# SyncE's order in the second recurrence: solved block out and back, next pair's blocks out, off-diagonal copies, blocks in

## The chip, the cores and the metric

The kernel runs on one core of a Trainium2 chip. Its time is the device time of one execution in microseconds. It was run three times, and the median counts. The profile is of one further execution, with its own time.

## What is computed

Batch 1, 512 positions, width 2048, float32. A first block (a modulated norm, a projection, sparse attention on 8 heads, a gated linear recurrence on 8 heads, an output projection) is followed by two layers: one of stick-breaking attention and pooling, and one whose core is this recurrence over time, on 32 heads of 64 channels:

```python
def step(state, inp):
    r_t, w_t, k_t, v_t, kk_t, a_t = inp
    sa = jnp.einsum('bhvk,bhk->bhv', state, -kk_t)
    state = (state * w_t[:, :, None, :]
             + sa[..., None] * (kk_t * a_t)[:, :, None, :]
             + v_t[..., None] * k_t[:, :, None, :])
    return state, jnp.einsum('bhvk,bhk->bhv', state, r_t)
```

It is the second recurrence of the title. A projection and a layer norm follow it. All else is unchanged and only takes its time before and after.

## The kernel before

Most of the kernel is matrix products: weights come from DRAM into `RAW`, ScalarE (ACT) and VectorE (DVE) split them in a high and a low part, and TensorE (PE) multiplies three times (L321 to L323). The second recurrence stands near the end, between the last group of such products and the output projection.

**Chunks and pairs.** Two heads make a pair of 128 channels, so there are 16 pairs (`PAIRS`), and the 512 positions are 8 chunks of 64. Within a chunk the update by `kk` and `a` couples the positions by a triangular 64 by 64 system, one for each chunk and head, so 16 systems in a pair. Each is inverted in three steps. First its four diagonal blocks of 16 by 16 are solved, by GpSimd (POOL). Then TensorE joins blocks of 16 to blocks of 32 ("level 5", l = 0 in `pe_level_w` and `pe_level_y`) and blocks of 32 to 64 ("level 6", l = 1), which takes the blocks next to the diagonal, copied out of the system to `T_N5` and `T_N6`. After that come products (`pe_pq`, `pe_fg`, `pe_oa`, `pe_gg`) and eight hops of the state from chunk to chunk (`pe_hop`, `dve_hop`).

**The systems' way.** `pe_nt` makes the systems of pair q in PSUM, and `act_nt` (L2105) copies them to SBUF and counts `nt_sb`. POOL works on another layout, one system to a partition, so everything goes over DRAM, all of it by DMAs that SyncE (SP) issues:
- `sp_blocks_out` (L1824) waits for `nt_sb` and writes the systems to `blocks_scratch` (2 DMAs);
- `sp_blocks_in` (L1830) waits until these have landed and reads the diagonal blocks to `SOLVE_IN` (2 DMAs);
- `pool_solve` waits for the solved block of the pair before to be out (`y_out`), sets the start (L1870), waits for the blocks (`n_in`) and runs 15 steps of two operations (L1876, L1879), the last of which counts `solved`;
- `sp_solved_out` (L1845) waits for `solved` and writes the solved block to `solved_scratch` (2 DMAs);
- `sp_solved_back` (L1851) waits until these have landed and reads them to `YT` in the layout of the products (2 DMAs); DVE's transpose `dve_inverse` (L2232) reads it next;
- `sp_levels` (L1839) waits for `w` (the level products of the pair before) and copies the blocks off the diagonal from the systems to `T_N5` (4 DMAs) and `T_N6` (2 DMAs).

Scratch tensors and `SOLVE_IN` have two buffers each; POOL's own working tiles have one.

**The order.** The loop is written out for iterations t, and each engine has a list of its own in which a step belongs to pair t, t+1 and so on: `at(t + 3, f, 1)` calls f for pair t+3 if that is a pair and at least 1. An engine goes through its list in order, and a wait stops all that is behind it. PE's list (`wv_pe`) begins with level 5's product of pair t+1 (L1956), has `pe_nt` of pair t+3 a few steps on, and the second L1956 (level 6) behind it. SP's list (`wv_sp`) has five entries an iteration, with 14 DMAs. Pair 0 goes through the five steps ahead of the loop, and pair 1's blocks go out and in at t = -2, where no other entry applies. The inputs of later pairs are loaded by ACT in its own list (L1801, L1808). POOL has only `pool_solve`, pair after pair.

Of the kernel before, what the change touches and what calls it, by code (L numbers as in the profile page):

```python
# [108 lines left out]
def wait(eng, sem, value):  # L109

    if not isinstance(value, int) or value > 0:
        eng.wait_ge(sem, value)
# [7 lines left out]
def build(nc, xT, positions, cols_d, mats_d, causal_i_d, rows_d, band_d, wpool_d, lora_d, lora1_d, kw_d, ada_d, gate_d, w_d, out):  # L120
    ctx = ExitStack()
    with ctx:
# [16 lines left out]
        at = (nc.sbuf_base + 31) // 32 * 32  # L139
# [1562 lines left out]
        def ws(i, n=1):  # L1702

            buf, first = ((WS, 0) if i < 48 else (X, 48) if i < 64 else (RAW[0], 64) if i < 68 else (GATE[i - 68], i)
                          if i < 70 else (WK, 54))
            return buf[:, (i - first) * SEQ:(i - first + n) * SEQ]
# [103 lines left out]
        def by_row(a, r):  # L1810

            return a.rearrange("(z y) -> z y", y=8 * DIAG)[:, r * 4 * DIAG:r * 4 * DIAG + CH * CH].rearrange(
                "z (p i) -> p z i", i=CH)

        def by_block(a):

            return a.rearrange("(x y) -> x y", y=DIAG)[:, 0:BASE16 * CH].rearrange("x (j i) -> x j i", i=CH)[
                :, :, 0:BASE16]

        def sp_blocks_out(sp, q):  # L1820

            sp.wait_ge(wv("nt_sb"), q + 1)
            for r in range(2):
                sp.dma_start(by_row(n_d[q % 2], r), ws(N_OF(q))[rows(r)].rearrange("p (z i) -> p z i", i=CH)  # L1824
                             ).then_inc(wv("n_out"), 16)

        def sp_blocks_in(sp, q):
            sp.wait_ge(wv("n_out"), 32 * (q + 1))
            for g in range(2):
                sp.dma_start(SOLVE_IN[q % 2][rows(g)], by_block(n_d[q % 2])).then_inc(wv("n_in"), 16)  # L1830

        def sp_levels(sp, q):

            wait(sp, wv("w"), 2 * q)
            for l, w in ((5, 16), (6, 32)):
                for b in range(P // (2 * w)):
                    at, to = b * 2 * w, (b * 2 * w) % CH + w
                    view = lambda i: ws(i)[at:at + w, :].rearrange("p (z i) -> p z i", i=CH)[:, :, to:to + w]
                    sp.dma_start(view(T_N5 if l == 5 else T_N6), view(N_OF(q))  # L1839
                                 ).then_inc(wv("levels" if l == 5 else "levels6"), 16)  # L1840

        def sp_solved_out(sp, v):
            sp.wait_ge(wv("solved"), v + 1)
            for g in range(2):
                sp.dma_start(by_block(y_d[v % 2])[:, g:BASE16:2, :], SOLVED[rows(g)]).then_inc(wv("y_out"), 16)  # L1845

        def sp_solved_back(sp, v):
            sp.wait_ge(wv("y_out"), 32 * (v + 1))
            wait(sp, wv("pq"), 2 * (v - 1))
            for r in range(2):  # L1850
                sp.dma_start(YT(v)[rows(r)].rearrange("p (z i) -> p z i", i=CH), by_row(y_d[v % 2], r)  # L1851
                             ).then_inc(wv("y_in"), 16)

        def at(p, f, first=0):

            if first <= p < PAIRS:
                f(p)

        def wv_sp(sp, t):
            at(t + 3, lambda q: sp_blocks_out(sp, q), 1)  # L1860
            at(t + 2, lambda q: sp_solved_out(sp, q), 1)
            at(t + 3, lambda q: sp_blocks_in(sp, q), 1)
            at(t + 2, lambda q: sp_solved_back(sp, q), 1)
            at(t + 2, lambda q: sp_levels(sp, q), 1)

        def pool_solve(pool, v):

# [476 lines left out]
        def _(sp):  # L2344
# [81 lines left out]
            for t in range(-2, PAIRS):  # L2426
                wv_sp(sp, t)
# [748 lines left out]
```

## Time and profile before

| | us |
|---|---|
| median of three runs | 3448.85 |
| lowest and highest | 3445.24, 3454.91 |
| profiled execution, its time | 3452.13 |
| profiled execution, its span | 3450.4 |
| TensorE busy | 3308.2 |
| POOL busy | 423.9 |

The span is from the first to the last instruction in the profile. Busy is the time in which an engine works on an instruction; waits and the issuing of DMAs are not in it. In the profile "SPq" is SyncE issuing, "ACTq" ScalarE issuing.

### The profile page before, as it was taken

To read this page: it belongs to the slowest core of one execution; us is meant where nothing else is said; L and a number is where in the kernel's file an instruction comes from. 1 tells how busy PE (TensorE), PEld (TensorE's weight loads), DVE (VectorE), ACT (ScalarE), POOL (GpSimd) and SP (SyncE) were. 2 spreads that over 40 slices of the span, in tenths; PEclk is the share of its full clock that TensorE was granted. 3 is DMA by queue.
4 is the path that set the end of the run, shared out by engine and by line. 5 is a ranking of instruction groups with operands and counts; after the bars stand their busy time and mean duration, and the time that the engine had idled before them with its cause. 6 is when DMAs were issued, how large, how long until landed. Compare 5 with 4: busy or idle time off the path is not lost.

```text
span 3450.4 us, 51304 instructions
## 1 busy us (share of the span) xinstructions
PE 3308.2 (96%) x20966; PEld 2682.0 (78%) x20966; DVE 1844.9 (53%) x2416; ACT 1356.9 (39%) x1587; POOL 423.9 (12%) x804
## 2 busy tenths in 40 slices
PE   6999999999999999999999999999999997889897
PEld 1678888888887888888888867888888886777785
DVE  7666666666667233444423456242456435667545
ACT  2343544443444133444422236242445533444323
POOL 0001223132221000000000000000010113434000
PEclk9999999999999999999999999999999998999898
DMA  9422232233322432222222314444464555554321
GB/s 387 164 79 93 88 106 94 88 114 105 109 100 89 165 134 86 85 81 86 80 88 104 123 55 159 146 138 140 161 233 161 213 176 142 124 135 105 134 98 73
DMA packets 200156, 435.18 MB, mean 126 GB/s; under 512 B 114608, under 2 KB 118064, under 8 KB 166192
## 3 DMA queue, kind: packets, MB, share of 16 engines
q1 hardware_dynamic: 153536, 311.00, 26.6%
q0 software_dynamic: 21872, 77.67, 6.6%
q10 hardware_dynamic: 24576, 44.05, 4.0%
q8 instruction: 127, 2.08, 0.2%
q14 instruction: 45, 0.37, 0.0%
HBM read 370.80 MB, written 60.29 MB: 125 GB/s over the span
## 4 chain that ended last, share of the span: by engine, by line
PE 88%; DVE 5%; ACT 2%; issue 1%; DMA 1%; SPq 1%; ACTq 1%; POOLq 1%; DVEq 0%; POOL 0%
PE PJ L321 18%; PE PJ L323 18%; PE PJ L322 18%; PE AB L321 6%; PE AB L323 6%; PE AB L322 6%; PE AB L1956 1%; PE AB L1965 1%; PE PJ L1977 1%; PE AB L2027 1%; DMA WK<-ada 1%; PE PJ L1892 1%; PE AB L256 1%; PE AB L495 1%; PE AB L547 1%
## 5 line engine op out<-in xcount | busy, mean ns | idle before, releaser
L321 PE MATMUL PJ<-XH,WH 128*128 128x512 f32 x2816 | 1112.2, 395 | 15.0 <-DVE XL L469 7.6
L323 PE MATMUL PJ<-XH,WL 128*128 128x512 f32 x2816 | 1098.9, 390 | 0.0
L322 PE MATMUL PJ<-XL,WH 128*128 128x512 f32 x2816 | 1098.7, 390 | 0.0
L354 DVE TENSOR_TENSOR WL<-RAW,WH 128x2048 fp32r<-128x2048 f32 (+1 forms) x234 | 539.2, 2304 | 639.4 <-ACT WH L350 635.4
L350 ACT ACTIVATE WH<-RAW 128x2048 fp32r<-128x2048 f32 (+1 forms) x236 | 449.4, 1904 | 783.7 <-PE PJ L323 547.6
L321 PEld LDWEIGHTS PJ<-XH,WH 128*128 128x128 f32 x2816 | 530.1, 188 | 125.5 <-issue 17.5
L323 PEld LDWEIGHTS PJ<-XH,WL 128*128 128x128 f32 x2816 | 529.8, 188 | 111.8
L322 PEld LDWEIGHTS PJ<-XL,WH 128*128 128x128 f32 x2816 | 530.3, 188 | 108.7 <-issue 2.2
L321 PE MATMUL AB<-XH,WH 128*128 128x512 f32 (+1 forms) x960 | 380.0, 396 | 11.6 <-DVE XL L469 7.6
L323 PE MATMUL AB<-XH,WL 128*128 128x512 f32 (+1 forms) x960 | 375.3, 391 | 0.0
L322 PE MATMUL AB<-XL,WH 128*128 128x512 f32 (+1 forms) x960 | 375.2, 391 | 0.0
L321 PEld LDWEIGHTS AB<-XH,WH 128*128 128x128 f32 (+1 forms) x960 | 179.2, 187 | 55.2 <-issue 11.5
L322 PEld LDWEIGHTS AB<-XL,WH 128*128 128x128 f32 (+1 forms) x960 | 179.3, 187 | 41.9 <-issue 2.4
L323 PEld LDWEIGHTS AB<-XH,WL 128*128 128x128 f32 (+1 forms) x960 | 179.2, 187 | 40.1 <-issue 0.8
L659 POOL TENSOR_TENSOR TBL<-GATE,SMALL 128x512 f32<-128x512 f32 x16 | 30.3, 1892 | 485.5 <-PE AB L674 242.8
L663 POOL TENSOR_TENSOR TBL<-TBL,GATE 128x512 f32<-128x512 f32 x48 | 79.6, 1659 | 77.6 <-issue 76.2
L487 DVE COPY WK<-PJ 128x1024 f32<-128x1024 f32 x30 | 36.7, 1224 | 90.9 <-PE PJ L323 90.9
L256 PE MATMUL AB<-WK,SMALL 128*1 128x512 f32 x128 | 63.4, 635 | 21.9 <-DMA WK<-ada 21.8
L2481 POOL DMA_DIRECT2D TBL<-wpool x4 | 2.2, 546 | 593.0 <-DVE X L1376 444.4
L1876 POOL TENSOR_TENSOR X<-X 128x30 f32<-128x30 f32 (+10 forms) x240 | 66.9, 279 | 60.8 <-DMA X<-blocks_scratch 27.7
L1879 POOL TENSOR_TENSOR X<-X 128x30 f32<-128x30 f32 (+10 forms) x240 | 69.9, 291 | 35.2 <-issue 1.9
L1956 PE MATMUL AB<-WS 64*64 64x64 f32 x1024 | 39.7, 232 | 26.1 <-DVE WS L2242 10.9
(537 smaller groups left out, 3932.7 us busy)
## 6 DMA issues: line engine op xcount, KB each, us to landing
RAW<-w SPq DMA_DIRECT2D x232, 1024.0 KB, 4.8
WK<-ada SPq DMA_DIRECT2D x32, 1024.0 KB, 6.7
GATE<-gate POOLq DMA_DIRECT2D x64, 256.0 KB, 2.9
rkvg_scratch<-WK POOLq DMA_DIRECT2D x16, 1024.0 KB, 5.0
factors_scratch<-WK POOLq DMA_DIRECT2D x48, 256.0 KB, 2.9
X<-factors_scratch ACTq DMA_DIRECT2D x35, 256.0 KB, 4.0
x_scratch<-X POOLq DMA_DIRECT2D x8, 1024.0 KB, 5.7
rates_scratch<-WK POOLq DMA_DIRECT2D x16, 512.0 KB, 4.6
```

The lines of the kernel that those rows point to most:

```text
L256: m = nc.tensor.matmul(AB[0:1, 2 + b, :], SILU[:, SKT * k + j:SKT * k + j + 1], WK[:, at:at + SEQ], start=k == 0 and j == 0, stop=False)
L321: nc.tensor.matmul(bank[0:width, n, :], hi, xh, start=first, stop=False)
L322: nc.tensor.matmul(bank[0:width, n, :], hi, xl, start=False, stop=False)
L323: m = nc.tensor.matmul(bank[0:width, n, :], lo, xh, start=False, stop=last)
L350: nc.scalar.activation(WH[k % 2][:, :, 0:w], narrow(RAW[k % 2], w), ACT.Copy).then_inc(wh_ready, 1)
L354: nc.vector.tensor_tensor(WL[k % 2][:, :, 0:w], narrow(RAW[k % 2], w), WH[k % 2][:, :, 0:w].bitcast(F32), ALU.subtract).then_inc(wl_ready, 1)
L487: nc.vector.tensor_copy(WK[:, n0 * SEQ:n1 * SEQ].rearrange("p (b n) -> p b n", n=SEQ), PJ[:, n0:n1, :]).then_inc(evac_d, 1)
L495: m = nc.tensor.transpose(dst[:, t * P:(t + 1) * P], src[:, t * P:(t + 1) * P], mat("ident"))
L663: m = nc.gpsimd.tensor_tensor(GATE_ACC, GATE_ACC, GATE[k % 2][:, :], ALU.add)
L1876: P_TT(SCRATCH[:, 0:c, 0:w], n[:, j:j + 1, j + 1:].to_broadcast([P, c, w]), SOLVED[:, 0:c, j:j + 1].to_broadcast([P, c, w]), ALU.mult)
L1879: m = P_TT(SOLVED[:, 0:c, j + 1:], SOLVED[:, 0:c, j + 1:], SCRATCH[:, 0:c, 0:w], ALU.subtract)
L1956: i = nc.tensor.matmul(tok(bank(4), r, m, h), tok(ws(T_N6 if l else T_N5), r, m, h), tok(ws(T_X), r, m, h), start=True, stop=True)
```

## The change

SP's five entries of an iteration come in another order. What each does, waits for and counts is as before, and so are the steps ahead of the loop and all other engines' lists.

```diff
         def wv_sp(sp, t):
+            at(t + 2, lambda q: sp_solved_out(sp, q), 1)
+            at(t + 2, lambda q: sp_solved_back(sp, q), 1)
             at(t + 3, lambda q: sp_blocks_out(sp, q), 1)
-            at(t + 2, lambda q: sp_solved_out(sp, q), 1)
+            at(t + 2, lambda q: sp_levels(sp, q), 1)
             at(t + 3, lambda q: sp_blocks_in(sp, q), 1)
-            at(t + 2, lambda q: sp_solved_back(sp, q), 1)
-            at(t + 2, lambda q: sp_levels(sp, q), 1)
```

## Rows read from the trace of the kernel before

**Rows 1.** The page: the chain that ended last, by engine.

```profile
PE 88%; DVE 5%; ACT 2%; issue 1%; DMA 1%; SPq 1%; ACTq 1%; POOLq 1%; DVEq 0%; POOL 0%
```

**Rows 2.** A window: length, busy PE, PEld, DVE, ACT, POOL, clock, DMA, GB/s.

```profile
2820.00:3223.00 403.00, 347.70 (x7578) 298.27 (x7580) 252.14 (x429) 160.05 (x284) 144.97 (x500) 0.94 0.49 122
```

**Rows 3.** The chain of waits: start, length, piece, in us.

```profile
3011.21 0.93 PE AB L1956 x32
...
3053.70 2.09 issue
...
3206.78 1.07 PE AB L1956 x32
```

**Rows 4.** POOL in order of time: operations that begin or end a solve.

```profile
2869.71 0.21 POOL L1876 TENSOR_TENSOR X<-X 128x15 f32<-128x15 f32 x1 [11.01 <-DMA X<-blocks_scratch]
...
2882.92 0.22 POOL L1879 TENSOR_TENSOR X<-X 128x8 f32<-128x8 f32 x1
...
2890.10 0.21 POOL L1876 TENSOR_TENSOR X<-X 128x15 f32<-128x15 f32 x1 [0.39 <-DMA X<-blocks_scratch]
...
2901.34 0.22 POOL L1879 TENSOR_TENSOR X<-X 128x8 f32<-128x8 f32 x1
...
3191.59 0.22 POOL L1879 TENSOR_TENSOR X<-X 128x8 f32<-128x8 f32 x1
```

**Rows 5.** Waits in the loop (in total, times, longest); last L2232's own (in total, times).

```profile
SPq L1824 <- ACT WS L2105: 113.2, 14, 10.4
...
POOL X L1870 <- DMA solved_scratch<-X: 100.9, 13, 11.6
...
POOL X L1876 <- DMA X<-blocks_scratch: 16.3, 13, 2.8
...
PE AB L1956 <- issue: 7.7, 4, 2.2
...
  DMA WS<-solved_scratch: 6.8, 1
```

**Rows 6.** SP's issues in order of time: start, length, line, DMA, count.

```profile
2852.62 1.30 SPq L1845 DMA_DIRECT2D solved_scratch<-X  x2
2858.37 1.29 SPq L1851 DMA_DIRECT2D WS<-solved_scratch  x2
2859.70 1.31 SPq L1824 DMA_DIRECT2D blocks_scratch<-WS  x2
2865.39 1.31 SPq L1830 DMA_DIRECT2D X<-blocks_scratch  x2
...
2890.67 3.90 SPq L1839 DMA_DIRECT2D WS<-WS  x6
...
3016.41 1.30 SPq L1824 DMA_DIRECT2D blocks_scratch<-WS  x2
...
3025.98 4.51 SPq L1839 DMA_DIRECT2D WS<-WS  x6
...
3191.84 1.30 SPq L1845 DMA_DIRECT2D solved_scratch<-X  x2
3196.23 1.28 SPq L1851 DMA_DIRECT2D WS<-solved_scratch  x2
```

**Rows 7.** Landing of one DMA, of L1845 (solved out), then L1830 (blocks in).

```profile
DMA to landing us min/median/max: 2.1/3.9/6.6
...
DMA to landing us min/median/max: 2.5/3.5/5.1
```

**Rows 8.** Windows of three iterations, and of one iteration's first 2 us.

```profile
3033.45:3055.79 22.34, 19.12 (x480) 16.40 (x475) 16.97 (x30) 10.05 (x19) 9.56 (x32) 0.98 0.58 145
3055.79:3080.71 24.92, 21.87 (x478) 18.96 (x479) 16.26 (x28) 9.85 (x18) 8.73 (x30) 0.88 0.51 120
3146.47:3166.72 20.25, 19.11 (x484) 16.50 (x482) 16.31 (x30) 9.85 (x19) 9.54 (x32) 1.00 0.43 96
...
3055.00:3057.00 2.00, 1.21 (x23) 1.25 (x25) 0.00 (x0) 0.00 (x0) 1.14 (x5) 0.50 0.06 14
```

## The prediction, made before the changed kernel ran

> **What bounds the kernel now.** I read the page first, then the stretch of the second recurrence by windows, POOL's and SyncE's (SP's) instructions in order of time, the waits, and last the chain of waits. The chain that ended last lies 88% on TensorE [rows 1]. That average says little of the edited loop. The second recurrence runs from 2820 to 3223 us, 403 of 3450 us, with TensorE busy 347.7 us, POOL 145.0 us, and the DMA engines at half their share [rows 2]. The edit touches nothing outside it.
>
> Inside it the reader is to see two circles. The first is the compute circle, from one first L1956 (level 5's product) to the next, through PE, DVE and ACT: 22.34 us in a middle iteration (3033.45 to 3055.79), 20.25 us in a late one (3146.47 to 3166.72) where the loads of later pairs have ended [rows 8]. The second is the solve circle: SP carries a pair's blocks to DRAM and back, POOL solves them, SP carries the solved block out and back. POOL's solve takes 13.4 us for pair 1 (2869.71 to 2883.14) and 11.5 for pair 2 (2890.10 to 2901.56) [rows 4]. Its mean comes from the waits: between the ends of solve 2 and of solve 15 (3191.81) POOL idles 100.9 us until a solved block is out and 16.3 until blocks are in, 13 times each [rows 4, 5]; (290.25 - 117.2) / 13, less a copy of 0.3 us, is 13.0 us. So POOL is idle 40% of this stretch. The fourteen solves after solve 1 end on average 22.05 us apart, (3191.81 - 2883.14) / 14 [rows 4]: they keep the compute circle's pace and have slack. SP has slack too: in 14 waits it stands 113.2 us for ACT's copy of the systems, `nt_sb` [rows 5], which in the order of before is ahead of everything, the solved block included. But that block's return is not late: DVE's L2232, its first reader, waits for it once, 6.8 us [rows 5]. What is nearly late is the off-diagonal copies, SP's last step. PE stops 7.7 us in four places before L1956 with no releaser in the trace [rows 5], 2.09 us of them at 3053.70 [rows 3], and I count these as waits for those copies, the only input of L1956 that a DMA brings in itself.
>
> **The change, part by part.** No instruction is added or taken away: SP issues the same 14 DMAs an iteration, each now behind others.
>
> *Solved out and back come ahead of the wait for `nt_sb`.* They can leave when POOL ends. Nothing waits for them today, so this is worth 0.
>
> *Blocks out goes behind the wait for the solved block to land, and blocks in goes last.* This is what counts. In the order of before the next pair's blocks are already on their way while the solved block is, and blocks in is issued ahead of the wait for that landing. In the new order all that lies between two solves stands in one line. From the end of one solve to the end of the next:
> 1. Solved out issued and landed: 5.4 us. Rows: 5.75 (2852.62 to 2858.37), and 4.4 with no loads about (3191.84 to 3196.23) [rows 6]; the second DMA leaves 0.65 after the first and lands 2.1 / 3.9 / 6.6 us later [rows 7], so at most 7.3. I stay near the first row, because most iterations have loads beside them.
> 2. Solved back, two issues: 1.3 us [rows 6]. SP doesn't wait for its landing.
> 3. Blocks out, two issues: 1.3 us [rows 6]. `nt_sb` is there: it comes 5.2 us after L1956 begins (3011.21 to 3016.41) [rows 3, 6], and that L1956 begins some 12 us after the solve before.
> 4. Off-diagonal copies, six issues: 4.5 us (3.9 at 2890.67) [rows 6]. Their wait for `w`, on an L1956 a few us after the iteration's first, is also long past. They cover the landing of blocks out: that took 5.7 us from issue to blocks in (2859.70 to 2865.39) [rows 6], against 1.3 + 4.5 = 5.8 here.
> 5. Blocks in, until POOL's first operation: 4.4 us. Rows: 4.3 (2865.39 to 2869.71) [rows 4, 6]; 0.65 and a landing of 2.5 / 3.5 / 5.1 [rows 7] make 3.2 / 4.2 / 5.8.
> 6. The solve: 13.0 us; 11.5 to 13.4 [rows 4].
>
> The sum is 29.9 us. With the low end of each it is 4.4 + 1.3 + 1.3 + 3.9 + 4.2 + 11.5 = 26.6, with the high end 7.3 + 1.3 + 1.3 + 4.5 + 5.8 + 13.4 = 33.6. The trace of before holds one such circle, at the loop's start, where nothing overlaps yet: solved out 2852.62, solved back 2858.37, blocks out 2859.70, blocks in 2865.39, the solve until 2883.14 [rows 4, 6]. That is 30.5 us, without step 4 but with a full landing of 5.7 us in place of steps 3 and 4. It is the row nearest to my sum.
>
> This circle sets the pace then: 29.9 against 22.05 us. It begins after solve 1, since pair 1's blocks go out and in as before. Fourteen circles: 14 x 7.85 = 109.9 us.
>
> *The end.* From the last solve (3191.81) to the last first-L1956 (3206.78) it takes 15.0 us today, because compute is late there [rows 3, 4]. Then SP will be: 4.4 + 1.3, four of the six copies issued in 2.6, and a landing of 2 to 4 us [rows 6, 7], 11 in all: a gain of 4.0.
>
> *What the new idle time costs.* TensorE ends an iteration's work and stands some 5 us before each first L1956. Its granted clock is 0.50 (1.2 GHz) at 3055 to 3057, behind the stop of 2.09 us, and 0.88 in the mean over that iteration, so it came back to 2.4 GHz within it [rows 3, 8]. The iteration took 24.92 against 22.34 us before it, so 2.6 us [rows 8]. Beside a circle of 29.9 that is hidden; it would count if the circle were under 25. In the last iteration nothing hides it: + 2.4.
>
> Sum: 109.9 - 4.0 + 2.4 = 108.3 us; the profiled execution's 3452.1 + 108.3 = 3560.4. The median of the runs shown is 3.3 us below that execution, so I say **3557**.
>
> The rows above show no pair of solved-out DMAs that landed in under 4.4 us from the first issue. The Trainium skill ("DMA: Bandwidth & Descriptors", Anatomy of one DMA) gives a DMA a fixed cost of about 2 us, mostly the receipt of its last write. By that, steps 1 and 5 would take 2.65 us each, the circle would be 25.4, and the whole some 3496. No run here shows that for such short runs of data; a result near it falls below the range.
>
> **The rivals.**
> - *A short circle.* DMAs that today share the queues land alone. For it: the 4.4 us of the last solved out, the 11.5 of solve 2. Against: the loads of later pairs are still there in most iterations, and the circle at the start took 30.5. With every low end: 14 x (26.6 - 22.05) - 2 = + 62, so 3511.
> - *Compute on the slow clock throughout.* If the clock never came back, TensorE, busy 19.1 of the 20.25 us [rows 8], would need twice as long. With three quarters of the circle on it, that makes 35 us an iteration, 14 x 13 = + 182, so 3631. Against: the clock came back within one iteration after the stop [rows 8]. The Trainium skill ("TensorE: Matmul & The Clock Gate", Part 1) calls the throttled state the default, lifted by activity; if a busy share of 19 us in 30 didn't lift it, this is the case that follows.
> - *Faster: the copies come in time.* They leave right behind blocks out instead of 9.6 us after it (3016.41 to 3025.98) [rows 6]. If POOL's side keeps pace, the four stops before L1956 go, 7.7 us [rows 5], and with each 2.6 us of slow clock [rows 8]: - 18, so 3431. It decides at a circle of 22.05 us. Even the low ends miss it by 4.5; the solve would have to take 5 us instead of 13.
> - *No change.* The circle comes to about 22.5 us and its loss equals that gain. The same speaks against it.
>
> **How the numbers follow.** Forecast (a circle of 28 to 33 us) 0.83; short circle 0.07; slow clock 0.05; faster 0.03; no change 0.02. The last two bounds are at 0.3% (10 us), which is about what a measurement of this kernel tells from no change: slower 0.95, same 0.02, faster 0.03. The range: a circle of 27.3 us gives 3519 by the same sum, one of 32.3 gives 3589. I take 3514 to 3590, which leaves most of both outer rivals out.
>
> **What would show it.** In the profile after, solves end 28 to 33 us apart. POOL idles some 17 us between two solves, 5 before L1870 and 11 to 12 before L1876, for blocks coming in. SP's wait at L1824 for `nt_sb` is gone, and it waits for POOL at L1845 some 16 us each time. L1956 waits for the copies in every iteration, and the mean granted clock of the stretch falls under 0.94. Outside it nothing moves by over 2 us. The prediction is wrong if POOL starts solves less than 14 us after the last ended, or if iterations stay near 22 us.

## The result

The changed kernel took 3548.32 us (median of four runs, 3546.14 to 3550.76), the one before 3451.88 us on the same chip (the three runs above and a fourth): a ratio of 1.0276, with a 95% interval of 1.0248 to 1.0305. It is slower by some 96 us; 3557 was forecast, in 3514 to 3590. The profiled execution has a span of 3545.8 us, 95.4 more than before.

The page of the changed kernel, the chain that ended last, by engine, answers to [rows 1]:

```profile
PE 79%; DMA 5%; POOLq 4%; DVE 3%; SPq 3%; issue 3%; ACT 1%; DVEq 0%; ACTq 0%; POOL 0%
```

The chain has left TensorE for 9% of the span. Where it went is seen in the same view, of one circle between two solves' ends:

```profile
by line: POOLq L1878 18.6%; POOLq L1875 16.8%; issue 15.0%; SPq L1839 12.8%; DMA solved_scratch<-X 12.1%; DMA X<-blocks_scratch 10.8%; SPq L1824 4.4%; SPq L1851 4.2%; SPq L1845 4.2%; SPq L1830 2.1%; POOL X L1879 1.6%
```

Not one piece of it is TensorE's. The chain is POOL's solve, then each of SP's steps and two transfers. SP's issues in order of time, of that circle, answer to [rows 6]:

```profile
3032.47 1.29 SPq L1845 DMA_DIRECT2D solved_scratch<-X  x2
3036.64 1.27 SPq L1851 DMA_DIRECT2D WS<-solved_scratch  x2
3037.95 1.31 SPq L1824 DMA_DIRECT2D blocks_scratch<-WS  x2
3039.30 3.90 SPq L1839 DMA_DIRECT2D WS<-WS  x6
3043.25 1.34 SPq L1830 DMA_DIRECT2D X<-blocks_scratch  x2
3061.27 1.29 SPq L1845 DMA_DIRECT2D solved_scratch<-X  x2
```

POOL beside it, and the last operations of solve 1 and of solve 15, answer to [rows 4]:

```profile
2888.25 0.22 POOL L1879 TENSOR_TENSOR X<-X 128x8 f32<-128x8 f32 x1
...
3036.67 0.29 POOL L1870 COPY X<-MAT 128x128 f32<-128x128 f32 x1 [4.23 <-DMA solved_scratch<-X]
3047.19 0.21 POOL L1876 TENSOR_TENSOR X<-X 128x15 f32<-128x15 f32 x1 [10.23 <-DMA X<-blocks_scratch]
3061.03 0.22 POOL L1879 TENSOR_TENSOR X<-X 128x8 f32<-128x8 f32 x1
...
3289.59 0.22 POOL L1879 TENSOR_TENSOR X<-X 128x8 f32<-128x8 f32 x1
```

From solve 1 (2888.47) to solve 15 (3289.81) it is 28.67 us a circle, against 22.05. The waits answer to [rows 5], the first four of POOL and PE from 2900 to 3295, SP's and DVE's of the whole loop:

```profile
POOL X L1876 <- DMA X<-blocks_scratch: 149.8, 14, 11.8
...
PE AB L1956 <- issue: 56.8, 10, 8.4
...
POOL X L1870 <- DMA solved_scratch<-X: 51.4, 13, 5.9
...
PE AB L1956 <- DVE WS L2232: 14.2, 3, 5.2
...
SPq L1845 <- POOL X L1879: 243.1, 15, 17.0
SPq L1851 <- DMA solved_scratch<-X: 41.8, 16, 4.4
...
SPq L1824 <- ACT X L2105: 6.3, 1, 6.3
SPq L1830 <- DMA blocks_scratch<-WS: 6.3, 3, 4.7
...
  DMA WS<-solved_scratch: 60.7, 15
```

SP's 113 us of waiting for `nt_sb` are gone (the one left is ahead of the loop). It waits for POOL in their place, 16.2 us each time. POOL waits for its blocks, 10.7 us each time. TensorE stops ahead of the first L1956 in all fifteen iterations. The view puts three of the thirteen stops shown down to DVE's L2232, which reads the solved block, but L2232 had ended 0.7 to 0.9 us earlier there. The last of level 5's four copies lands 0.09 us ahead of L1956 in fourteen iterations and 0.14 us in the first: in the circle above it is issued at 3041.31 and lands 1.8 us later, and L1956 starts at 3043.21. So all these stops are waits for the copies. The windows answer to [rows 2, 8]:

```profile
2820.00:3320.00 500.00, 385.62 (x7719) 333.45 (x7721) 258.79 (x435) 164.11 (x292) 155.78 (x500) 0.84 0.40 99
...
3044.00:3046.00 2.00, 2.00 (x29) 1.76 (x25) 0.16 (x1) 0.60 (x1) 0.00 (x0) 0.50 0.49 53
3046.00:3048.00 2.00, 2.00 (x20) 1.76 (x20) 1.07 (x3) 0.60 (x1) 0.53 (x3) 0.50 0.30 28
...
3050.00:3052.00 2.00, 1.47 (x52) 1.23 (x44) 1.83 (x4) 0.84 (x2) 1.23 (x5) 1.00 0.00 0
```

The granted clock of the stretch fell from 0.94 to 0.84, because each iteration begins behind a stop of TensorE: L1956 starts at 3043.21 at 1.2 GHz and the clock is 2.4 GHz again from 3050.

### The profile page after: what moved, and what is told of

It is laid out like the page before. It is cut to its first block, busy times and chain, and to the rows that moved or that the text cites. A ratio compares the mean times of both kernels' runs of the same rounds, so it can differ in the third digit from the quotient of the medians.

```text
span 3545.8 us, 51304 instructions
## 1 busy us (share of the span) xinstructions
PE 3343.5 (94%) x20966; PEld 2713.4 (77%) x20966; DVE 1846.7 (52%) x2416; ACT 1356.4 (38%) x1587; POOL 434.0 (12%) x804
## 4 chain that ended last, share of the span: by engine, by line
PE 79%; DMA 5%; POOLq 4%; DVE 3%; SPq 3%; issue 3%; ACT 1%; DVEq 0%; ACTq 0%; POOL 0%
PE PJ L321 17%; PE PJ L323 17%; PE PJ L322 17%; PE AB L321 6%; PE AB L322 6%; PE AB L323 6%; POOLq L1878 2%; POOLq L1875 2%; DMA solved_scratch<-X 2%; DMA X<-blocks_scratch 1%; SPq L1839 1%; DMA WK<-ada 1%; SPq L1851 1%; SPq L1824 1%; PE AB L495 1%
## 5 line engine op out<-in xcount | busy, mean ns | idle before, releaser
L1956 PE MATMUL AB<-WS 64*64 64x64 f32 x1024 | 51.8, 274 | 87.7 <-issue 59.2
L1956 PEld LDWEIGHTS AB<-WS 64*64 64x64 f32 x1024 | 47.2, 184 | 92.8 <-issue 66.6
L1876 POOL TENSOR_TENSOR X<-X 128x30 f32<-128x30 f32 (+10 forms) x240 | 74.9, 312 | 194.3 <-DMA X<-blocks_scratch 161.1
L1879 POOL TENSOR_TENSOR X<-X 128x30 f32<-128x30 f32 (+10 forms) x240 | 72.4, 301 | 35.3 <-issue 1.9
```

Of the source, the lines that this page charges most:

```text
L1876: P_TT(SCRATCH[:, 0:c, 0:w], n[:, j:j + 1, j + 1:].to_broadcast([P, c, w]), SOLVED[:, 0:c, j:j + 1].to_broadcast([P, c, w]), ALU.mult)
L1879: m = P_TT(SOLVED[:, 0:c, j + 1:], SOLVED[:, 0:c, j + 1:], SCRATCH[:, 0:c, 0:w], ALU.subtract)
L1956: i = nc.tensor.matmul(tok(bank(4), r, m, h), tok(ws(T_N6 if l else T_N5), r, m, h), tok(ws(T_X), r, m, h), start=True, stop=True)
```

## The experiments

Each experiment but e4 and e5 moves entries of SP's list, and each ratio is to the kernel before on the same chip. "Circle" is the mean over the fourteen solves after solve 1, from end to end; "solve" is the mean of POOL's own part. Both are read from the profiled execution, the time from all runs.

| run | order after the exchange | us | ratio (95%) | circle | solve |
|---|---|---|---|---|---|
| before | blocks out, solved out, blocks in, back, copies | 3448.9 to 3458.5 | 1 | 22.05 | 12.9 |
| changed | solved out, back, blocks out, copies, blocks in | 3548.3 | 1.0276 (1.0248 to 1.0305) | 28.67 | 13.7 |
| e1 | solved out, back, blocks out, blocks in, copies | 3530.0 | 1.0231 (1.0214 to 1.0249) | 28.04 | 12.6 |
| e2 | blocks out, solved out, back, copies, blocks in | 3521.0 | 1.0197 (1.0180 to 1.0214) | 27.22 | 13.8 |
| e3 | solved out, blocks out, blocks in, back, copies | 3476.1 | 1.0070 (1.0053 to 1.0087) | 23.94 | 12.8 |
| e4 | as changed, 5 of 15 solve steps | 3441.2 | 0.9951 (0.9937 to 0.9965) | 20.92 | 4.2 |
| e5 | as before, 5 of 15 solve steps | 3457.4 | 1.0005 (0.9991 to 1.0019) | 21.93 | 4.0 |
| e6 | blocks out, solved out, blocks in, 4 copies, back, 2 copies | 3485.2 | 1.0086 (1.0057 to 1.0114) | 24.79 | 12.5 |
| e7 | blocks out, solved out, 4 copies, blocks in, back, 2 copies | 3463.5 | 1.0025 (1.0008 to 1.0043) | 23.12 | 13.5 |
| e8 | blocks out, 4 copies, solved out, blocks in, back, 2 copies | 3440.0 | 0.9951 (0.9932 to 0.9970) | 21.26 | 13.7 |
| e9 | blocks out, 6 copies, solved out, blocks in, back | 3453.6 | 1.0000 (0.9981 to 1.0020) | 21.87 | 13.7 |

**e1: do the copies cost, or only cover?** Against the changed kernel:

```diff
-            at(t + 2, lambda q: sp_levels(sp, q), 1)
             at(t + 3, lambda q: sp_blocks_in(sp, q), 1)
+            at(t + 2, lambda q: sp_levels(sp, q), 1)
```

> The changed order with its last two entries exchanged: blocks in ahead of the off-diagonal copies. My theory: the copies stand in the circle but cover the landing of blocks out (some 5.5 us from issue), so that blocks in can't leave sooner: solves 28.2 to 29.3 us apart (28.7 changed), time 3540 to 3560. Rival, that the six copies' issues (4.1 us) are themselves what blocks in waits for: solves 24.6 us apart, time near 3491.

The circle is just under the range and the time 10 us under it, far from the rival's 24.6 and 3491. Blocks in leaves on average 4.8 us after blocks out, where it left after 5.8 with the copies between: they cover most of the landing, but are not free by 1.0 us. What is gained there, blocks in loses on its way (4.7 us to POOL's first operation in place of 3.9, with the copies issued right behind it), and solved out lands 0.5 us later. The solve is 1.1 us shorter, for which the last section has the likely cause. Fourteen circles shorter by 0.63 us make 9 us. The two profiled executions are 18.9 us apart; another 7.0 of these lie ahead of the end of solve 1, which the exchanged entries don't touch, and 3.2 behind solve 15.

**e2: only blocks in last.** Against the changed kernel:

```diff
+            at(t + 3, lambda q: sp_blocks_out(sp, q), 1)
             at(t + 2, lambda q: sp_solved_out(sp, q), 1)
             at(t + 2, lambda q: sp_solved_back(sp, q), 1)
-            at(t + 3, lambda q: sp_blocks_out(sp, q), 1)
             at(t + 2, lambda q: sp_levels(sp, q), 1)
             at(t + 3, lambda q: sp_blocks_in(sp, q), 1)
```

> Order: blocks out, solved out, solved back, copies, blocks in. Blocks out leaves early as before; only blocks in stays behind the solved block's way and the copies. Theory (a serial circle): only the two issues of blocks out leave it, 28.7 - 1.35 = 27.3 us, time near 3529 (3515 to 3540). Rival, that what costs is blocks out standing behind the wait for the solved block to land: then the loss goes with it, 22 to 23 us, 3450 to 3465.

27.22 us against 27.3 forecast: from solved back to blocks in it takes 5.8 us in place of 7.2, and nothing else moves by over 0.3 us. SP's issues in one circle of it, in order of time:

```profile
3026.56 1.25 SPq L1845 DMA_DIRECT2D solved_scratch<-X  x2
3030.35 1.27 SPq L1851 DMA_DIRECT2D WS<-solved_scratch  x2
3031.66 3.90 SPq L1839 DMA_DIRECT2D WS<-WS  x6
3035.61 1.33 SPq L1830 DMA_DIRECT2D X<-blocks_scratch  x2
3043.23 1.29 SPq L1824 DMA_DIRECT2D blocks_scratch<-WS  x2
3053.87 1.25 SPq L1845 DMA_DIRECT2D solved_scratch<-X  x2
```

Blocks out waits beside the solve here and costs nothing; what stands between solved out and blocks in does. The rival's 22 to 23 us are far off.

**e3: the landing not waited for.** Against the kernel before:

```diff
+            at(t + 2, lambda q: sp_solved_out(sp, q), 1)
             at(t + 3, lambda q: sp_blocks_out(sp, q), 1)
-            at(t + 2, lambda q: sp_solved_out(sp, q), 1)
             at(t + 3, lambda q: sp_blocks_in(sp, q), 1)
```

> Order: solved out, blocks out, blocks in, solved back, copies. Solved out is first as in the change, but its landing isn't waited for ahead of blocks in. Theory: the circle is 1.3 (solved out) + 5.2 (blocks out landed) + 3.9 (blocks in) + 13.3 (solve) = 23.7 us, so time 3452 + 14 x 1.7 = 3476 (3462 to 3495). Rival, that solved out ahead of nt_sb is harmless or even good, since compute sets the pace: 22 us, 3445 to 3455.

3476.1 us and a circle of 23.94: as forecast. Solved out ahead of blocks out already costs 0.7%, because blocks out's landing then lies in POOL's circle; SP's wait for solved out's landing and the copies cost the other 2%.

**e4 and e5: the solve shortened.** The changed order and the one before, each with a solve that is left unfinished:

```diff
-            for j in range(BASE16 - 1):
+            for j in range(5):
```

> The changed order, but POOL does 5 of the solve's 15 steps (the solved blocks are left unfinished), some 4 us instead of 13.7. Theory: the circle falls to about 19 us, under compute's 20 to 22, so the whole loss goes and the off-diagonal copies come in time: the stops before L1956 go and the time is 3428 to 3442. Rival, that waiting for the solved block's landing ahead of blocks out costs by itself (SP held up, systems late): it stays 20 us or more above the kernel before.

> The order of before with the same 5 of 15 steps (the rest of the solve left out). Theory: in the order of before POOL has slack, and SP is held at nt_sb, not by POOL, so 3444 to 3453, and e4 is faster than this by 5 to 18 us, the worth of early copies. Rival, that the stops before L1956 are not waits for the copies: e4 and e5 within 4 us of each other.

With a solve of 4 us the changed order is faster than the kernel before, and 16 us faster than its counterpart e5. So nothing in this order costs by itself; it costs through a POOL circle that is longer than compute's. e5 shows that a faster POOL is worth nothing to the order of before (its time is over the range by 4 us, with the kernel before at 3458.5 on that chip; the ratio says no change). The stops before L1956, from 2900 to 3190, of e4 and then of e5:

```profile
PE AB L1956 <- issue: 5.3, 2, 3.0
```

```profile
PE AB L1956 <- issue: 9.1, 6, 3.1
```

Six stops become two, which is the gain that the faster rival named, and near its size (16 against 18 us). That such stops are waits for the copies had only been inferred, since the view names no releaser. The landings bear it out: the last of level 5's copies lands 0.09 us ahead of L1956 at each of e5's six stops, at e4's two, and at the four of the kernel before, while ahead of the other L1956 of e4 in this window it lands 2.4 to 9.1 us early.

**e6 and e7: a better place for the copies, first tries.** `sp_levels` got an argument that keeps it to level 5 (four DMAs) or level 6 (two). The lines behind it move down by 2 and then 3: in e6 to e8 L1841, L1847, L1853, L1959, L2235 and L2245 are what L1839, L1845, L1851, L1956, L2232 and L2242 are elsewhere. e6, against the kernel before:

```diff
             at(t + 3, lambda q: sp_blocks_in(sp, q), 1)
+            at(t + 2, lambda q: sp_levels(sp, q, 5), 1)
             at(t + 2, lambda q: sp_solved_back(sp, q), 1)
-            at(t + 2, lambda q: sp_levels(sp, q), 1)
+            at(t + 2, lambda q: sp_levels(sp, q, 6), 1)
```

> Order: blocks out, solved out, blocks in, level 5's four copies, solved back, level 6's two copies. POOL's circle stays as before (1.3 + 4.4 + 13 = 18.7 us), and what the next L1956 needs lands some 14 us after nt_sb instead of 17. Theory: the stops before L1956 and the slow clock behind them go: 3432 to 3446. Rival, that ACT and its loads set the pace and not the copies: 3449 to 3456.

e7 has the same with level 5's entry one further up, ahead of blocks in.

> Order: blocks out, solved out, level 5's four copies, blocks in, solved back, level 6's two copies. The four copies use the time in which blocks out lands, but stand in POOL's circle, 1.3 + 2.6 + 4.4 + 13 = 21.3 us, close to compute's 20 to 22. Theory (any circle near 22 costs again): no better than e6, 3436 to 3456. Rival, that only the long circle of the change costs: 3 us or more faster than e6.

e6 was wrong in sign. I had moved the copies some 3 us earlier and solved back behind them, and counted 2.6 us for their four issues. They take 3.9 us in the mean. The iteration shown has 5.07, and solved back leaves 10.9 us after blocks out, where it left after 8.3 in the kernel before:

```profile
3004.10 1.30 SPq L1824 DMA_DIRECT2D blocks_scratch<-WS  x2
3005.45 1.34 SPq L1847 DMA_DIRECT2D solved_scratch<-X  x2
3008.46 1.32 SPq L1830 DMA_DIRECT2D X<-blocks_scratch  x2
3009.82 5.07 SPq L1841 DMA_DIRECT2D WS<-WS  x4
3014.99 1.99 SPq L1853 DMA_DIRECT2D WS<-solved_scratch  x2
```

And DVE's reader of the solved block (L2235), which waited once in the kernel before, for 6.8 us, now waits in most iterations, and PE's first L1959 for it. Waits of e6 from 2900 to 3190:

```profile
DVE WS L2235 <- DMA WS<-solved_scratch: 36.6, 11, 5.5
...
PE AB L1959 <- DVE WS L2235: 33.5, 10, 5.3
```

So the solved block's return had hardly more slack than the copies. In e7 SP issues four copies while blocks out lands. The same wait is 21.1 us in 6 cases, and POOL's circle holds the copies' issues, 23.12 us. At 3463.5 us it is over its range and 0.25% slower than before, but 22 us faster than e6: the expectation that it would be no better was wrong, and the rival's "3 us or more faster than e6" is what came.

**e8 and e9: level 5's copies, or all six, ahead of solved out.** e8, against the kernel before:

```diff
             at(t + 3, lambda q: sp_blocks_out(sp, q), 1)
+            at(t + 2, lambda q: sp_levels(sp, q, 5), 1)
             at(t + 2, lambda q: sp_solved_out(sp, q), 1)
             at(t + 3, lambda q: sp_blocks_in(sp, q), 1)
             at(t + 2, lambda q: sp_solved_back(sp, q), 1)
-            at(t + 2, lambda q: sp_levels(sp, q), 1)
+            at(t + 2, lambda q: sp_levels(sp, q, 6), 1)
```

> Order: blocks out, level 5's four copies, solved out, blocks in, solved back, level 6's two copies. The four copies fill the time in which blocks out lands, and stand ahead of solved out, so out of POOL's circle (18.7 us). Blocks in leaves when before, 5.3 us after nt_sb, and solved back 8.4 us after it (8.3 before). Theory: the waits for the copies go and nothing else gets late: 3434 to 3447, as e4 against e5. Rival, that solved out 2.6 us later makes its return the late one, as in e6: 3456 or more.

> Order: blocks out, all six copies, solved out, blocks in, solved back. As e8, with 1.3 us more ahead of solved out: its return reaches DVE some 15 us after nt_sb, 20.2 us after L1956, where the late iterations are 20.25 us long. Theory: 3436 to 3452, at best as e8 and up to 8 us slower. Rival, as for e8: 3458 or more.

e8 took 3440.0 us, a ratio of 0.9951 (0.9932 to 0.9970). SP's issues of e8 in one iteration:

```profile
3032.37 1.30 SPq L1824 DMA_DIRECT2D blocks_scratch<-WS  x2
3033.72 3.80 SPq L1841 DMA_DIRECT2D WS<-WS  x4
3037.56 1.29 SPq L1847 DMA_DIRECT2D solved_scratch<-X  x2
3038.90 1.35 SPq L1830 DMA_DIRECT2D X<-blocks_scratch  x2
3040.71 1.25 SPq L1853 DMA_DIRECT2D WS<-solved_scratch  x2
```

Blocks in leaves 6.5 us after blocks out, where 5.3 was expected, and solved back 8.3 us after it, as expected. Between solved out and blocks in nothing stands, so POOL's circle has its slack, and the copies use time in which SP stood waiting for a landing. PE's waits of e8, 2900 to 3190, first of the second L1959 for its own input, then of the first for the solved block:

```profile
PE AB L1959 <- DVE WS L2245: 8.5, 13, 1.5
...
PE AB L1959 <- DVE WS L2235: 2.4, 3, 1.4
```

The stops without a releaser are gone, and the circle is 21.26 us: this order is 0.5% faster than the one before, with the whole interval below 1. e9, with level 6's two copies ahead as well, gave 3453.6 and no difference from before; that is 2 us over its range. It differs from e8 by the two copies' 1.3 us ahead of solved out. Its profiled execution, 3443.1 us, is with the fastest of its twelve (up to 3468.0), so its trace tells little of the median. In it the first L1956 waits for the solved block in six cases, 5.5 us, against 2.4 in three for e8:

```profile
PE AB L1956 <- DVE WS L2232: 5.5, 6, 2.4
```

That points to the solved block's return, now 1.3 us later, but that it takes the whole of the 13 us back is not shown.

## Why the prediction was right

The mechanism held in every part that the runs could try: no TensorE in the chain between solves, SP in one line, the pace that of POOL's circle. The experiments take it apart. Blocks out's issues alone are worth 1.4 us a circle (e2), and against e3 solved back, the wait for the landing ahead of it and the copies are worth 4.7 (e3); a short solve turns the sign (e4). The sum was 13 us too high on the profiled execution, 108.3 against 95.4, and part of that closeness is luck: the fourteen circles were put 17 us too high, and 5 us that chance added at the loop's start made up for some of it:

- **Step 1, solved out landed: 5.4 us, measured 3.9** (mean of the fourteen; 4.17 at 3032.47). This is the term most off. I stayed near the circle at the start, where it took 5.75, and took 4.4 for a low end. Twelve of the fourteen came in under that end, four of them in 2.8 us. The rows had allowed it: the shortest single landing, 2.1 us, behind the second issue makes 2.75. The Trainium skill's fixed cost of about 2 us ("DMA: Bandwidth & Descriptors", Anatomy of one DMA) is given there for DMAs that GpSimd issues, and these are SP's. Those four are near it, with 2.2 us behind the second issue, but the mean, with 3.3, is not.
- **Steps 2 to 4**: 7.1 us, measured 7.2. The wait for `w` and the one for `nt_sb` were long past, and SP waited for blocks out's landing at L1830 three times, 6.3 us in all. That the copies cost nothing beside it was a little too kind (1.0 us, e1).
- **Step 5**: 4.4 us, measured 3.9 (3.7 to 4.1). The low end of 4.2 was the median of the rows, not their shortest, 3.2. With the shortest of steps 1 and 5 the sum of low ends is 24.0, not 26.6, so the short circle was a nearer rival than it was made out.
- **Step 6, the solve**: 13.0 us, measured 13.7 in the mean, over the highest row that I had for it, 13.4. See the last section.
- Together 28.7 for 29.9, so 92.7 us for 109.9.
- **The end**: 3289.81 to L1956's start at 3300.19 is 10.4 us, and 11 was said; the gain is 4.6 in place of 4.0. From that L1956 to the end of the span it takes 1.9 us more than before (245.6 against 243.7), where 2.4 was put down to the slow clock. The granted clock is 0.77 in the first 22 us before and 0.64 changed; how much of the 1.9 us is the clock's is not settled:

```profile
3206.70:3228.70 22.00, 17.68 (x356) 14.67 (x352) 9.40 (x18) 9.56 (x16) 0.00 (x0) 0.77 0.18 69
3300.19:3322.19 22.00, 17.67 (x338) 15.37 (x338) 7.41 (x13) 7.53 (x12) 0.00 (x0) 0.64 0.33 112
```

- **Outside the loop nothing moves by over 2 us: wrong.** Solve 1 ends 5.3 us later than before, and this is in the 95.4. The start of the loop isn't changed; in the full-solve experiments solve 1 ends anywhere from 2880.9 to 2887.7. Executions differ by that much, and the forecast should have allowed it.
- **Small slips**: by the sum's own rule the circle of 25.4 us gives 3494 and not 3496, and circles of 27.3 and 32.3 give 3521 and 3591, not 3519 and 3589. "28 to 33 us" and "27.3 to 32.3" were both called the forecast's circle; 28.67 lies in both. The sign "less than 14 us" from one solve's end to the next one's start was touched once, with 13.96; the mean is 15.0.

Slow clock throughout: didn't happen. The granted clock was 2.4 GHz again 3.6 to 8.7 us after L1956's start in thirteen iterations, 12.1 us after it in the last but one and 15.8 in the last. Compute with a slow start stayed under the circle, as TensorE's mean stop of 5.5 us (71.0 in 13) shows. The rival "faster" named a true gain, but one that needs an order in which POOL keeps its pace.

## What to carry to other kernels

Where one in-order queue serves two circles, as SP's does for POOL's and compute's, write out for each circle what stands between its own two steps, waits on landings included, and add it to the engine's work: a circle's slack is gone when that sum passes the pace of the others, however idle the engine looks (POOL was idle 40% of the stretch here). Fill a queue's wait for a landing with issues that belong to neither circle's short side. Slack measured on one transfer says nothing of its neighbour's: e6 took the time from one late transfer and made the next one late.

## What the runs showed of the hardware

POOL's operations on SBUF stretch beside some of DVE's. POOL and then DVE of the changed kernel, in order of time:

```profile
3051.66 0.25 POOL L1876 TENSOR_TENSOR X<-X 128x36 f32<-128x36 f32 x1
3052.06 0.61 POOL L1879 TENSOR_TENSOR X<-X 128x36 f32<-128x36 f32 x1
3052.82 0.61 POOL L1876 TENSOR_TENSOR X<-X 128x32 f32<-128x32 f32 x1
3053.57 0.25 POOL L1879 TENSOR_TENSOR X<-X 128x32 f32<-128x32 f32 x1
```

```profile
3051.81 0.75 DVE L2276 SCALAR_TENSOR_TENSOR X<-X,COL,WS 128x512 f32<-128x512 f32 x1
3052.64 0.69 DVE L2281 TENSOR_TENSOR WK<-X,WS 128x512 f32<-128x512 f32 x1
3053.37 0.69 DVE L2222 TENSOR_TENSOR WS<-AB,MAT 128x512 f32<-128x512 f32 x1
```

Beside L2276 and L2281, whose inputs both lie in SBUF, an operation of 0.25 us takes 0.61; beside L2222, with an input in PSUM, it takes 0.25. From 2895 to 3215 us, 64 of the 330 operations of this kind in the changed kernel took over 0.4 us, none of the 53 without a DVE operation beside them, and all 20 that touched L2281. They cost some 26 us more there than at 0.25 us each. The eleven profiled executions agree. Of the 4060 operations of their solves 2 to 15, 999 overlap a DVE operation other than a transpose whose inputs all lie in SBUF, and 631 of these take over 0.4 us; of the other 3061, beside nothing, a transpose or an operation with an input in PSUM, none takes over 0.27.

How many are slow depends on where SP's order puts the solve beside DVE's list, and the solve's length goes with it:

| runs | slow operations in a solve | solve, us |
|---|---|---|
| e1, e6 | 3.1, 3.4 | 12.6, 12.5 |
| before, e3 | 4.0, 4.0 | 12.9, 12.8 |
| changed, e2, e7, e8, e9 | 5.4 to 5.9 | 13.5 to 13.8 |

That is where the 0.8 us of the changed kernel's solve come from by the count; no run moved DVE's list to try it. The Trainium skill ("GPSIMD Engine Reference", Specifications) states contention with DVE instructions that have two SBUF inputs, and the trace agrees.
